# The MLP down projections of a two-layer decoder step: seven-product 2x2 block form in place of the plain product

## What is computed

```python
def sq_relu_mlp(h, w_up, w_down):
    u = jax.nn.relu(h @ w_up)
    return (u * u) @ w_down

x = x + mix
x = x + sq_relu_mlp(rmsnorm(x, w['norm_mlp'][l]), w['w_up'][l], w['w_down'][l])
```

## Time and profile before

| | |
|---|---|
| median of 3 runs | 2680.24 us (2679.75 to 2681.32) |
| profiled execution, first to last instruction | 2680.4 us |
| TensorE busy | 2611.6 us (97%), 20,942 matmuls |
| VectorE, ScalarE, GpSimd busy | 1510.4, 826.6, 69.6 us |
| mean granted TensorE clock | 0.990 |
| HBM traffic | 144.0 MB read, 36.2 MB written |

### The profile page before, as it was taken

One profiled execution on the slowest core, in us unless ns is written; L12 is line 12 of the kernel. 1 busy time (PEld: TensorE's weight loads), 2 busy tenths in 40 slices (PEclk: granted clock), 3 DMA queues, 4 the chain that ended last, 5 costly groups with the idle time before them and its releaser, 6 DMA issues.

```text
span 2680.4 us, 49462 instructions
## 1 busy us (share of the span) xinstructions
PE 2611.6 (97%) x20942; PEld 2485.0 (93%) x20942; DVE 1510.4 (56%) x3220; ACT 826.6 (31%) x1871; POOL 69.6 (3%) x92
## 2 busy tenths in 40 slices
PE   7999999998999999999999999998999999999997
PEld 6899999996699999999999998886899999999997
DVE  6777777777575444444444634656754444444445
ACT  5545444444142111211121413446521112111211
POOL 0000000000400000000000000004100000000000
PEclk9999999998999999999999999999999999999999
DMA  3111101134311111111111224426111111111111
GB/s 144 57 50 42 35 33 50 42 127 167 108 48 48 48 48 48 48 48 48 48 48 48 97 81 128 119 76 207 41 53 43 48 48 48 48 48 48 48 32 64
DMA packets 85456, 178.11 MB, mean 66 GB/s; under 512 B 21809, under 2 KB 49705, under 8 KB 84521
## 3 DMA queue, kind: packets, MB, share of 16 engines
q1 hardware_dynamic: 76233, 162.72, 18.5%
q10 hardware_dynamic: 9008, 12.26, 1.4%
HBM read 143.95 MB, written 36.24 MB: 67 GB/s over the span
## 4 chain that ended last, share of the span: by engine, by line
PE 84%; DVE 8%; ACT 2%; DMA 2%; issue 1%; POOL 0%; SPq 0%; ACTq 0%; DVEq 0%
PE psum L2128 19%; PE psum L2129 19%; PE psum L2130 19%; PE psum L2202 3%; PE psum L2203 3%; PE psum L2204 3%; PE psum L2403 2%; PE psum L2154 2%; PE psum L2674 1%; PE psum L2619 1%; PE psum L2696 1%; PE psum L2497 1%; PE psum L2620 1%; PE psum L2621 1%; DVE v_conv L1373 1%
## 5 line engine op out<-in xcount | busy, mean ns | idle before, releaser
L2128 PE MATMUL psum<-x_hi,w_hi 128*128 128x352 f32 (+1 forms) x1040 | 334.8, 322 | 0.0
L2129 PE MATMUL psum<-x_lo,w_hi 128*128 128x352 f32 (+1 forms) x1040 | 332.4, 320 | 0.0
L2130 PE MATMUL psum<-x_hi,w_lo 128*128 128x352 f32 (+1 forms) x1040 | 330.9, 318 | 0.0
L1163 DVE SCALAR_TENSOR_TENSOR w_lo<-w_raw,gains,w_hi 128x512 fp32r<-128x512 f32 x380 | 262.1, 747 | 43.7 <-ACT w_hi L633 43.6
L633 ACT ACTIVATE w_hi<-w_raw,gains 128x512 fp32r<-128x512 f32 x380 | 247.1, 714 | 123.0 <-DMA w_raw<-in_w 122.5
L2202 PE MATMUL psum<-x_hi,w_hi 128*128 128x352 f32 (+1 forms) x768 | 272.4, 355 | 2.7 <-DVE pre L1245 2.7
L2128 PE MATMUL psum<-u_hi_b,w_hi 128*128 128x352 f32 (+1 forms) x768 | 247.1, 322 | 0.0
L2128 PE MATMUL psum<-u_hi,w_hi 128*128 128x352 f32 (+1 forms) x768 | 246.8, 321 | 0.0
L2128 PE MATMUL psum<-x_hi_b,w_hi 128*128 128x352 f32 (+1 forms) x768 | 246.6, 321 | 0.0
L2203 PE MATMUL psum<-x_lo,w_hi 128*128 128x352 f32 (+1 forms) x768 | 245.8, 320 | 0.0
L2129 PE MATMUL psum<-x_lo_b,w_hi 128*128 128x352 f32 (+1 forms) x768 | 245.5, 320 | 0.0
(11 more groups left out here) (379 smaller groups left out, 5459.3 us busy)
## 6 DMA issues: line engine op xcount, KB each, us to landing
w_raw<-in_w SPq DMA_DIRECT2D x190, 512.0 KB, 3.7
q_tile<-scratch_q SPq DMA_DIRECT2D x24, 256.0 KB, 3.1
scratch_att<-o_out ACTq DMA_DIRECT2D x32, 132.0 KB, 2.8
x<-in_x SPq DMA_DIRECT2D x8, 516.0 KB, 9.7
s_state<-in_s_rec_in SPq DMA_DIRECT2D x2, 2048.0 KB, 15.1
out_s_rec<-s_state SPq DMA_DIRECT2D x8, 512.0 KB, 2.6
merge<-scratch_att SPq DMA_DIRECT2D x8, 512.0 KB, 3.8
dec<-scratch_gates ACTq DMA_DIRECT2D x7, 512.0 KB, 3.5
```

What stands on the lines that cost most here:

```text
L1163: done = v.scalar_tensor_tensor(w_lo[:, slot, 2 * part + k], w_raw[:, part, k], gains[:, unit * UW + 2 * part + k:unit * UW + 2 * part + k ...
L2128: mm(out, whi, xh[:, k, cols], start=k == 0, stop=False)
L2129: mm(out, whi, xl[:, k, cols], start=False, stop=False)
L2130: done = mm(out, wlo, xh[:, k, cols], start=False, stop=k == kts - 1)
```

## The change

Of the 8 blocks of a layer, the 6 in the middle (`MIDDLE`) get a new form, and the last block's up product too.

- Tokens are cut into quarters of 258 columns. An up product's tile of 128 hidden features is made for two quarters at a time (g = 0, 1), one bank each, and VectorE takes the two banks in one operation of 516 columns. ScalarE now squares.
- The down product of a block (hidden 512 = 2 x 2 slices of 128, output 1,024, tokens 4 quarters) is made as 2x2 blocks: output tiles `quad` and `quad + 4`, two halves of K, two quarters of the tokens. Instead of 8 block products, 7 are made from sums of weight blocks (S1, S2, S4 and a difference) and of activation blocks (T1, T2, T4 and a difference). Products that appear in several results are accumulated on in PSUM: 6, 7 and 4 run on in product 1's bank pair, 3 in product 5's, and each intermediate sum is added to x by VectorE (`take_sum`) before the next product goes on top of it (`CHAIN`). There are 4 quads a block.
- The order of issue in quad 0 of a block is 1, 5, quad 1's 1, 6 and 2 interleaved by g, 3, 7, 4; in the others 1, 5, 6, 3, 7, 2, 4 (quad 1 without its 1).
- The weights of the middle blocks come in up tiles (1,024 x 128, 512 KB) and quads (four blocks of 256 x 128, 512 KB). GpSimd makes the sums of weight blocks (`quad_sums`) and all low parts there (`lo_tile`, `lo_quad`); ScalarE makes the high parts. Rings of two (high) and three (raw and low) hold them, in the place of the old ring.
- VectorE makes the sums of the activation blocks and their low parts (`middle`).
- The gain of the MLP's norm is multiplied into x (`x_prepare`) instead of the weights; weights without a gain are split by plain copies and subtractions. The table of gains is 136 columns instead of 384.
- Semaphores of earlier stages are used again under new names (`REUSED`).

```diff
+FIRST_ORDER = ((0, 1), (0, 5), (1, 1), (0, 6), (0, 2), (0, 3), (0, 7), (0, 4))
+SUMS = FIRST_ORDER + tuple((quad, p) for quad in range(1, 4) for p in (1, 5, 6, 3, 7, 2, 4) if (quad, p) != (1, 1))
+ISSUE = tuple((quad, p, g) for quad, p, g in (
+    (0, 1, 0), (0, 1, 1), (0, 5, 0), (0, 5, 1), (1, 1, 0), (1, 1, 1), (0, 6, 0), (0, 2, 0), (0, 6, 1), (0, 2, 1),
+    (0, 3, 0), (0, 3, 1), (0, 7, 0), (0, 7, 1), (0, 4, 0), (0, 4, 1))) + tuple((quad, p, g) for quad, p in SUMS[8:] for g in range(2))
+W_OF = {1: 3, 2: 5, 3: 2, 4: 6, 5: 0, 6: 1, 7: 4}
+U_OF = {1: 0, 2: 3, 3: 4, 4: 6, 5: 1, 6: 2, 7: 5}
+SUM_TO = {1: (0, 0), 2: (0, 0), 6: (0, 1), 3: (0, 1), 5: (1, 1), 7: (1, 1), 4: (1, 0)}
+SUM_AFTER = {2: 1, 3: 6, 7: 5}
+CHAIN = {6: 1, 3: 5, 7: 6, 4: 7}
...
+def sum_pair(block, quad, p):
+    w0, w1, w2, w3 = pair_turn(block)
+    if p in (5, 3):
+        return BANK_PAIRS[w1]
+    return BANK_PAIRS[(w0, w2, w3)[(quad - (p == 2)) % 3]]
...
+        def tile_weights(layer, t_):
+            if t_ > 2:
+                sp.wait_ge(sem("up_full"), tile_done(layer, t_ - 3))
+            sp.dma_start(t_raw[:, t_ % 3].rearrange("p k n -> p (k n)"), t["w_up"][:, layer * TILES + t_]
+            ).then_inc(sem(f"tile{t_ % 3}_landed"), L.add(f"tile{t_ % 3}_landed", 16))
+        def quad_weights(layer, d):
+            if d > 2:
+                sp.wait_ge(sem("sum_full"), quad_done(layer, d - 3))
+            sp.dma_start(d_raw[:, d % 3, 3:7].rearrange("p a k n -> p (a k n)"), t["w_quad"][:, layer * QUADS + d]
+            ).then_inc(sem(f"tile{3 + d % 3}_landed"), L.add(f"tile{3 + d % 3}_landed", 16))
...
+        def middle_weights(layer, unit):
+            sp.wait_ge(sem("u_ready"), L.next("u_ready", 12))
+            L.skip("u_ready", 8)
+            for t_ in range(3):
+                tile_weights(layer, t_)
+            sp.wait_ge(sem("up_full"), tile_done(layer, 0))
+            for d in range(3):
+                quad_weights(layer, d)
+            for b in range(MIDDLE):
+                for t_ in range(4 * b + 3, 4 * b + 7):
+                    tile_weights(layer, t_)
+                for d in range(4 * b + 3, min(4 * b + 7, QUADS)):
+                    quad_weights(layer, d)
+            sp.wait_ge(sem("sum_full"), quad_done(layer, QUADS - 1))
+            for part in range(2):
+                weight(unit + 4, part)
+            tile_weights(layer, TILES - 1)
+            for part in range(2):
+                weight(unit + 5, part)
...
         def x_prepare(third, k):
-            act.activation(lay.hi[:, k, THIRDS[third]], lay.x[:, k, THIRDS[third]], ACT.Copy
+            act.activation(lay.hi[:, k, THIRDS[third]], lay.x[:, k, THIRDS[third]], ACT.Copy,
+                           scale=1.0 if x_gain is None else gains[:, x_gain + k:x_gain + k + 1]
             ).then_inc(sem("x_hi_ready"), L.add("x_hi_ready"))
...
+        def hi_tile(layer, t_):
+            act.wait_ge(sem(f"tile{t_ % 3}_landed"), L.next(f"tile{t_ % 3}_landed", 16))
+            if t_ > 1:
+                act.wait_ge(sem("up_full"), tile_done(layer, t_ - 2))
+            act.activation(t_hi[:, t_ % 2], t_raw[:, t_ % 3], ACT.Copy).then_inc(sem("tile_hi_ready"), L.add("tile_hi_ready"))
+        def hi_quad(layer, d):
+            act.wait_ge(sem("quad_sums_ready"), L.next("quad_sums_ready"))
+            if d > 1:
+                act.wait_ge(sem("sum_full"), quad_done(layer, d - 2))
+            for part in (slice(0, 4), slice(4, 7)):
+                act.activation(d_hi[:, d % 2, part], d_raw[:, d % 3, part], ACT.Copy
+                ).then_inc(sem("quad_hi_ready"), L.add("quad_hi_ready"))
+        def square_up(layer, block, j, ap):
+            act.wait_ge(sem("up_taken"), evicted(layer, block, j))
+            act.activation(ap, ap, ACT.Square).then_inc(sem("squared"), L.add("squared"))
+        def hi_parts(layer, slot, *parts):
+            for part in parts:
+                act.wait_ge(sem("u_sums_ready"), L.next("u_sums_ready"))
+                act.activation(c_hi[layer][slot][:, part], c_raw[layer][slot][:, part], ACT.Copy
+                ).then_inc(sem("c_hi_ready"), L.add("c_hi_ready"))
+        def middle(layer, b):
+            for n in range(4):
+                hi_tile(layer, 4 * b + n + 1)
+                if b == 0 and n == 2:
+                    hi_quad(layer, 0)
+                if n == (1 if b else 3):
+                    hi_quad(layer, 4 * b + 1)
+                for g in range(2):
+                    slot = n // 2 * 2 + g
+                    raw = c_raw[layer][slot]
+                    if n % 2 == 0:
+                        square_up(layer, b, 2 * n + g, raw[:, 0:6:5])
+                        hi_parts(layer, slot, slice(0, 2))
+                    else:
+                        square_up(layer, b, 2 * n + g, raw[:, 3:5])
+                        hi_parts(layer, slot, slice(2, 5), slice(5, 7))
+            for d in range(4 * b + 2, min(4 * b + 5, QUADS)):
+                hi_quad(layer, d)
...
+        def lo_tile(t_):
+            pool.wait_ge(sem("tile_hi_ready"), L.next("tile_hi_ready"))
+            pool.tensor_tensor(t_lo[:, t_ % 3], t_raw[:, t_ % 3], f(t_hi[:, t_ % 2]), ALU.subtract
+            ).then_inc(sem("tile_ready"), L.add("tile_ready"))
+        def quad_sums(d):
+            pool.wait_ge(sem(f"tile{3 + d % 3}_landed"), L.next(f"tile{3 + d % 3}_landed", 16))
+            s1, s2, s4, a00, a10, a01, a11 = (d_raw[:, d % 3, n] for n in range(7))
+            pool.tensor_tensor(s1, a10, a11, ALU.add).then_inc(sem("pool_order"), L.add("pool_order"))
+            pool.wait_ge(sem("pool_order"), L.value("pool_order"))
+            pool.tensor_tensor(s2, s1, a00, ALU.subtract).then_inc(sem("pool_order"), L.add("pool_order"))
+            pool.tensor_tensor(a10, a00, a10, ALU.subtract).then_inc(sem("pool_order"), L.add("pool_order"))
+            pool.wait_ge(sem("pool_order"), L.value("pool_order"))
+            pool.tensor_tensor(s4, a01, s2, ALU.subtract).then_inc(sem("quad_sums_ready"), L.add("quad_sums_ready"))
+        def lo_quad(d):
+            for part in (slice(0, 4), slice(4, 7)):
+                pool.wait_ge(sem("quad_hi_ready"), L.next("quad_hi_ready"))
+                pool.tensor_tensor(d_lo[:, d % 3, part], d_raw[:, d % 3, part], f(d_hi[:, d % 2, part]), ALU.subtract
+                ).then_inc(sem("quad_ready"), L.add("quad_ready"))
+        def mlp():
+            lo_tile(0)
+            for b in range(MIDDLE):
+                for n in range(4):
+                    lo_tile(4 * b + n + 1)
+                    if b == 0 and n == 2:
+                        quad_sums(0)
+                        lo_quad(0)
+                        quad_sums(1)
+                    if n == (1 if b else 3):
+                        lo_quad(4 * b + 1)
+                        quad_sums(4 * b + 2)
+                for d in range(4 * b + 2, min(4 * b + 5, QUADS)):
+                    lo_quad(d)
+                    if d + 1 < QUADS:
+                        quad_sums(d + 1)
+            for n in range(3):
+                lo_tile(4 * MIDDLE + n + 1)
...
+        def take_up(layer, block, j, out):
+            n, g = divmod(j, 2)
+            v.wait_ge(sem("up_full"), L.next("up_full"))
+            v.scalar_tensor_tensor(out, bank_pair(BANK_PAIRS[pair_turn(block)[j % 4]]), 0.0,
+                                   rs[:, 2 * QUARTER * g:2 * QUARTER * (g + 1)].rearrange("p (t c) -> p t c", t=2), ALU.max, ALU.mult
+            ).then_inc(sem("up_taken"), L.add("up_taken"))
+            v.wait_ge(sem("squared"), L.next("squared"))
+        def lo_part(layer, slot, part):
+            v.wait_ge(sem("c_hi_ready"), L.next("c_hi_ready"))
+            v.tensor_tensor(c_lo[layer][slot][:, part], c_raw[layer][slot][:, part], f(c_hi[layer][slot][:, part]), ALU.subtract
+            ).then_inc(sem("u_split_ready"), L.add("u_split_ready"))
+        def take_sum(layer, b, quad, p):
+            half, t_ = SUM_TO[p]
+            out = lay.x[:, quad + 4 * half].rearrange("p (g t c) -> p t g c", g=2, t=2)[:, t_]
+            v.wait_ge(sem("sum_full"), L.next("sum_full"))
+            if p in SUM_AFTER:
+                v.wait_ge(sem("sum_taken"), summed(layer, b, quad, SUM_AFTER[p]))
+            v.tensor_tensor(out, out, bank_pair(sum_pair(b, quad, p)), ALU.add).then_inc(sem("sum_taken"), L.add("sum_taken"))
+        def middle(layer, b):
+            for j in range(8):
+                n, g = divmod(j, 2)
+                slot = n // 2 * 2 + g
+                raw = c_raw[layer][slot]
+                b00, t1, t2, b10, b11, b01, t4 = (raw[:, m] for m in range(7))
+                if n % 2 == 0:
+                    take_up(layer, b, j, raw[:, 0:6:5])
+                    v.tensor_tensor(raw[:, 1:3], o3(b01, 2), o3(b00, 2), ALU.subtract
+                    ).then_inc(sem("u_sums_ready"), L.add("u_sums_ready"))
+                    lo_part(layer, slot, slice(0, 2))
+                    continue
+                take_up(layer, b, j, raw[:, 3:5])
```

(81 more changed lines are left out.)

213 lines of the change are left out of this document (156 added, 57 removed).

## The result

The changed kernel takes 2660.87 us (median of 4 runs, 2656.57 to 2665.89), the kernel before 2680.78 beside it: a ratio of 0.9926, 95% interval 0.9913 to 0.9939. It is faster, by 19.9 us, half of the 39 that were forecast, though the time lies in the range. The profiled run is the shortest of the four, 2656.57 us with a span of 2654.7.

What follows compares the result with a forecast made beforehand. TensorE, 97% busy, was taken to bound the kernel. Middle blocks -43.9, last up products +0.6 and block 0 +4 summed to -39.3 us from 2680.4, giving 2641 us, range 2626 to 2664.

Steps and rivals of the forecast that it cites:

- The bound and the sign: Whole kernel: TensorE bounds it, with VectorE, ScalarE, GpSimd and DMA hidden in the middle blocks; faster given 0.90.
- The price of a matmul: MLP products: a matmul of 258 columns costs 118.6 ns, making a block's up product 0.31 us longer.
- rival 2: 258-column matmuls cost more from displaced rows: 2688 us (6%), or in the smaller case 2649 us (6% more).
- one line more: Middle-block matmuls: displaced rows cross one more 16-byte SBUF line each, the smaller case of rival 2, near 2649 us.
- The down product: Each middle block: 336 matmuls plus 42 further groups at 12 ns take 40.35 us against 45.37, saving 5.02.
- The wait before product 4: Quad 0's down product: TensorE stands still while VectorE takes product 7's sum, costing 1.05 us once a block.
- Rival 1: Down products: VectorE's 516-column sum outlasts one product, so four waits a quad stall; 2687 us, 4%.
- Rival 4: Down products: further waits with no product between, each 12.6 us over the kernel, giving 2654 us; 4%.
- The start of the down phase: Middle blocks: product 1's sum and the last tile's low part stay hidden, by 0.5 and 1.1 us.
- Its aside: Start of the down phase: without quad 1's moved product, one stall of nearly 1 us and one of 0.3.
- Block 0: First block of each layer: GpSimd meeting VectorE makes j = 7 late, costing 2 us a layer, +4 in all.
- Rival 3: GpSimd meeting VectorE costs more: 20 us a layer in block 0 (2677), or reaching other blocks (2665); 10%.

Runs made afterwards that it cites:

- the sums earlier: Changed kernel with GpSimd making quad 0's sums one tile earlier in block 0 and quad 2's sums held until tile 3 is finished; 2653.93 us, ratio 0.9889.
- Freeing j = 6: Changed kernel with GpSimd in block 0 doing quad 0 and 1 work earlier, then silent until tile 3 ends; 2649.98 us, ratio 0.9890.
- the last hold: Version with GpSimd silent and product 5 moved, but GpSimd in block 0 held until product 5 of quad 0 instead of tile 3; 2635.85 us, ratio 0.9828.
- the run that should have shown it: Kernel with quads prepared one tile earlier in block 0, plus ScalarE's square of j = 4 held until tile 2 is finished; 2658.50 us in one run.
- product 5 moved: Kernel with the sums earlier, plus quad 1's product 5 issued between products 7 and 4 of quad 0; 2641.14 us, ratio 0.9846.
- preparation one tile earlier: Changed kernel with block 0's preparing of the quads on ScalarE and GpSimd moved one tile earlier; 2654.44 us, ratio 0.9904.

## Why the prediction was half right

The gain is half of the forecast. Two terms of the sum were wrong, block 0 by 10.8 us and the price of a matmul by 6.3; what bounds the kernel, and where a middle block waits and for how long, were right.

**The bound and the sign** were right: TensorE alone set the time, VectorE (46 us of a block's 87, forecast 42), ScalarE (24, forecast 26), GpSimd (39, forecast 38) and the DMA stayed hidden in blocks 1 to 5.

**The price of a matmul** was mis-sized. The up phase gives 45.99 / 384 = 119.8 ns where 118.6 were taken. The two MLP rows carried on gave 119.2; pulling the value toward the 264-column row made it worse. Over 14 up phases it is 0.45 x 14 = 6.3 us. The small case of rival 2 is not the cause: in block 1's up phase the matmuls of the displaced quarters follow each other at 119.6 ns, those of the aligned ones at 119.9. The page "SBUF — State Buffer" of the Trainium skill (Specifications) has a penalty for each crossing to a new 16-byte line. The prediction's "one line more" was a miscount: 1,032 bytes touch 65 such lines from offset 0 and from offset 8 alike, so these runs neither bear out that penalty nor contradict it.

**The down product** was forecast at 40.35 and takes 40.36 without stops, but that is luck, two errors that cancel: 1.2 ns too little for each of 336 matmuls (0.40 us), and 12 ns for each of 42 further groups (0.50) where (40.36 - 336 x 0.1198) / 42 = 2.6 ns are seen. The difference between up and down was small and no price of a group.

**The wait before product 4** was right in place, number and size (1.04, forecast 1.05). Rival 1 fell: the sum of 516 columns from two banks takes 0.69 us. Rival 4 fell: no further wait in blocks 1 to 5. **The start of the down phase** held there too. Its aside, that without the moved product there would be a stall of nearly 1 us and a second of 0.3, was right for the first (0.91 from start to start, 0.63 of it idle), and the second did not come.

**Block 0** is the step that failed: "I take 2 us a layer, between 0 and 5". It was 7.4 in the profile and 8.5 when repeated, 10.8 us or more over the forecast of 4 for two layers. Seen rightly was the meeting, and that j = 7 would be late. Two parts were missed. First, ScalarE's queue, a wait that the step put at nothing: the copy of quad 0 waits for GpSimd's sums, which begin only behind the low part of a tile, and the squares of j = 4 and 5 stand behind the copy (5.5 us). The step counted what GpSimd does to VectorE's instructions, not what ScalarE's new wait does to those behind it. Second, the clock: a stop of 6 us is followed by 13 to 26 matmuls at half clock, 1.3 to 2.5 us. The meetings were as long as feared (2.62 and 1.88 us for operations of 0.42), but of the ten operations only the five of j = 6 were lengthened, by 4.8 us together: near the top of the 2 to 5 us of lateness that the step itself worked out, of which it then took 2. Rival 3's 20 us a layer was far too much.

**The sum.** -39.3, plus 6.3 for the matmuls (the up phases alone; in the down phases the two errors cancel), plus 10.8 for block 0, is -22.2, what the phases add up to in the trace. The runs lie up to 9 us apart around that; in the traces the stretch at half clock is worth up to 2.3 us of it, and the start of the first middle block up to 8.

How the stop of 6.16 us divides: with the late copy gone and the meetings as long as before (the sums earlier), VectorE's first sum came 3.8 us sooner, counted from the start of the up phase, and 2.35 us of stop were left. So in the presence of the meetings the late copy costs 3.8. Freeing j = 6 took away another 1.1 and freeing j = 7 0.5; 0.75 were left behind the last hold. The meetings of j = 4 and 5 stopped nothing once the copy was in time: in the run with the last hold they still lengthen VectorE's operations by 4.3 us, and no wait for the first sum is left.

What stays open: what the late copy would cost without any meeting, since the run that should have shown it held back nothing; and what moves the start of the first middle block by up to 8 us from run to run.

## What to carry to other kernels

Cost the first turn of a pipelined loop by itself, queue by queue: where one engine prepares in one phase what is otherwise spread over the phase before, ask for every new wait what stands behind it in that engine's list. A dependent chain over another engine had the same price in every block here (1.06 us there and back for 516 columns), and it took one independent product for each such chain: with one in hand for two chains the stop only changes its place. When an engine is held back to keep out of another's way, tie the release to that other engine's last instruction, not to the event that starts it. No run here did quite that: the holds tried let GpSimd go beside a VectorE operation with two SBUF inputs.

## What the runs showed of the hardware

- A VectorE operation with two SBUF inputs beside GpSimd's two-input operation lasted 2.62 us in place of 0.42, and 2.81 in place of 0.96; an addition from PSUM kept its 0.69. This is the exclusion for whole instructions that "SBUF — State Buffer" (Who interferes with whom) of the Trainium skill states. GpSimd loses less by it: its 1024-column subtraction takes 2.39 us alone and 2.41 in the mean, its sums of 256 columns 0.73 alone and up to 1.32 beside VectorE in the changed kernel.
- The granted clock was 0.50 (1.2 GHz) after a stop of 6.2 us of a TensorE that had been busy before, for 2.96 us in one execution and 5.75 in another of the same kernel. After stops of 2.3 us (sums earlier, alone and with product 5 moved) it stayed at 1.00 three times and fell once; after the four of 2.55 us (preparation one tile earlier, alone and with the square held) it fell three times.
- fp32r matmuls of 258 columns follow each other at 119.8 ns at full clock and at 214 at half: less than twice, so part of the 119.8 does not scale with the clock.
